# Another order around the biased score maps: scores earlier on PE, bias ahead of a division, even exponentials ahead of copies

## The reference, cut to what matters

```python
# a: 8 heads, plain softmax
sc = q @ k.T;  p = softmax(sc);  y = p @ v
# b: 8 heads, window of 128 keys to each side, bias by distance, and a sink
sc = where(valid, q @ k.T + bias, -1e30)
m  = max(max(sc, axis=-1), sink)
e  = exp(sc - m);  p = e / (sum(e) + exp(sink - m));  y = p @ v
# c: 4 heads with two maps each; the second is subtracted, scaled by lam
p = softmax(sc + bias);  y = (p[0] - lam * p[1]) @ v
...
gates  = sigmoid(h @ w_gates)            # 3 x 1024 columns
merged = sum over the three kinds of gates * (y @ w_branch)
```

## Time and profile before

| what | value |
|---|---|
| time, median of 3 executions | 2519.49 us (2513.41 to 2519.65) |
| the profiled execution: time / span | 2518.29 us / 2516.5 us |
| PE busy | 2479.6 us, 99% of the span |
| DVE, ACT, POOL busy | 1531.5, 1346.9, 255.5 us |
| DMA engines, share of the span on the main queue | 51.8% |
| chain that ended last, share by engine | PE 92%, DVE 4%, ACT 2%, issue 1% |

### The profile page before, as it was taken

One profiled execution on the slowest core, in us unless ns is written; L12 is line 12 of the kernel. 1 busy time (PEld: TensorE's weight loads), 2 busy tenths in 40 slices (PEclk: granted clock), 3 DMA queues, 4 the chain that ended last, 5 costly groups with the idle time before them and its releaser, 6 DMA issues.

```text
span 2516.5 us, 47973 instructions
## 1 busy us (share of the span) xinstructions
PE 2479.6 (99%) x19246; PEld 2312.7 (92%) x19246; DVE 1531.5 (61%) x2036; ACT 1346.9 (54%) x2077; POOL 255.5 (10%) x164
## 2 busy tenths in 40 slices
PE   9999999999999999999999999999999999999998
PEld 8989998999999999899989989799989988888997
DVE  5658756565565774656656556566555655567654
ACT  5447555544544664655555445665445445565543
POOL 0200220000000002100100001460000000354000
PEclk9999999999999999999999999999999999999999
DMA  6655414465655552348656555345555655434654
GB/s 235 207 186 172 136 67 160 143 197 195 198 198 193 168 166 70 126 142 228 205 178 202 194 177 161 110 145 187 188 189 186 195 193 168 135 111 167 201 188 139
DMA packets 118382, 428.10 MB, mean 170 GB/s; under 512 B 13164, under 2 KB 14956, under 8 KB 117804
## 3 DMA queue, kind: packets, MB, share of 16 engines
q1 hardware_dynamic: 117696, 424.82, 51.8%
q10 hardware_dynamic: 492, 0.46, 0.1%
HBM read 423.79 MB, written 1.44 MB: 169 GB/s over the span
## 4 chain that ended last, share of the span: by engine, by line
PE 92%; DVE 4%; ACT 2%; issue 1%; DMA 0%; ACTq 0%; SPq 0%; DVEq 0%; POOLq 0%
PE bank L483 41%; PE bank L694 39%; PE bank L503 2%; PE bank L1004 2%; PE bank L1708 1%; PE bank L1104 1%; DVE lo_slots L471 1%; PE bank L633 1%; PE bank L1725 1%; PE bank L1751 1%; PE bank L1895 1%; PE bank L1871 1%; DVE rope_mem L2108 1%; ACT hi_slots L457 0%; ACT probs L1790 0%
## 5 line engine op out<-in xcount | busy, mean ns | idle before, releaser
L471 DVE TENSOR_TENSOR lo_slots<-raw,hi_slots 128x1024 fp32r<-128x1024 f32 x732 | 901.1, 1237 | 696.3 <-ACT hi_slots L457 695.9
L457 ACT ACTIVATE hi_slots<-raw 128x1024 fp32r<-128x1024 f32 x788 | 830.7, 1058 | 737.2 <-PE bank L694 453.0
L694 PE MATMUL bank<-x_hi_room,hi_slots 128*128 128x256 f32 x2816 | 786.0, 279 | 1.7 <-DVE x_lo_room L663 1.2
L694 PE MATMUL bank<-x_lo_room,hi_slots 128*128 128x256 f32 x2816 | 784.1, 278 | 0.0
L694 PE MATMUL bank<-x_hi_room,lo_slots 128*128 128x256 f32 x2816 | 784.0, 278 | 0.0
L694 PEld LDWEIGHTS bank<-x_lo_room,hi_slots 128*128 128x128 f32 x2816 | 534.4, 190 | 0.1
L694 PEld LDWEIGHTS bank<-x_hi_room,hi_slots 128*128 128x128 f32 x2816 | 529.7, 188 | 3.9 <-issue 3.6
L694 PEld LDWEIGHTS bank<-x_hi_room,lo_slots 128*128 128x128 f32 x2816 | 530.0, 188 | 0.0
L483 PE MATMUL bank<-x_hi_room,hi_slots 128*128 128x256 f32 x1152 | 327.7, 285 | 1.9 <-DVE x_lo_room L663 1.4
L483 PE MATMUL bank<-x_lo_room,hi_slots 128*128 128x256 f32 x1152 | 319.7, 278 | 0.0
L483 PE MATMUL bank<-x_hi_room,lo_slots 128*128 128x256 f32 x1152 | 319.6, 277 | 0.0
(11 more groups left out here) (336 smaller groups left out, 3125.0 us busy)
## 6 DMA issues: line engine op xcount, KB each, us to landing
raw<-w_full SPq DMA_DIRECT2D x792, 512.0 KB, 4.1
bias_mem<-bias_rows SPq DMA_DIRECT2D x8, 288.0 KB, 6.4
mem<-mem_t SPq DMA_DIRECT2D x2, 1024.0 KB, 8.4
const<-consts SPq DMA_DIRECT2D x1, 1664.0 KB, 8.8
h<-x_t SPq DMA_DIRECT2D x2, 512.0 KB, 7.8
final<-finals SPq DMA_DIRECT2D x2, 512.0 KB, 6.4
out_t<-h SPq DMA_DIRECT2D x4, 256.0 KB, 2.7
bias_rows<-junk ACTq DMA_DIRECT2D x1, 384.0 KB
```

The source lines that it names most:

```text
L457: nc.scalar.activation(w_hi[s], raw[s][:, :], ACT.Copy).then_inc(hi_ready[s], 1)
L471: nc.vector.tensor_tensor(w_lo[s], raw[s][:, :], w_hi[s].bitcast(F32), ALU.subtract).then_inc(lo_ready[s], 1)
L694: mm = nc.tensor.matmul(out, lhsT=w[:, part], rhs=x[:, k, :], start=k == 0 and b % 2 == 0 and n == 0, stop=k == KT - 1 and b % 2 == 1 and ...
```

## The change

Three orders change; no instruction is added or taken away.

- PE: the scores of maps 10 and 11, 12 and 13, 14 and 15 (the pairs of b maps that follow a pair of b maps) are issued a step earlier, behind the values and ahead of that step's gate product.
- DVE: for the even maps 10, 12 and 14, the bias is added ahead of the division of the map before.
- ACT: at every even step, for all three kinds, the exponentials of map i come ahead of the copy of the transposed map and of the copy of the values.

```diff
         def pe_attention(E, maps):
             for i in range(len(maps) + 2):
-                if i < len(maps) and i % 2 == 0:
...
+                if i < len(maps) and i % 2 == 0 and not scores_early(maps, i):
+                    pe_scores(E, maps, i)
...
+                if scores_early(maps, i + 1):
+                    pe_scores(E, maps, i + 1)
                 for g in gates_at(E, i):
                     pe_gate(E, g)
...
+        def scores_early(maps, i):
+            return 2 <= i < len(maps) and i % 2 == 0 and maps[i - 1]["kind"] == maps[i]["kind"] == "b"
...
         def act_attention(E, maps):
+            for i in range(len(maps) + 3):
+                first = i % 2 == 0
+                if first:
+                    exponential(i)
+                turned(i)
+                values(i)
+                if not first:
+                    exponential(i)
                 for g in gates_at(E, i - 1):
                     act_gate(E, g)
...
         def dve_attention(E, maps):
             for i in range(len(maps) + 4):
+                if scores_early(maps, i):
+                    add_bias(i)
                 if 1 <= i <= len(maps):
...
...
-                    dve.wait_ge(sems["s_ps"], E.after("s_ps", i + 1))
-                    if m["kind"] in "bc":
...
+                    if m["kind"] == "a":
+                        dve.wait_ge(sems["s_ps"], E.after("s_ps", i + 1))
+                    else:
+                        if not scores_early(maps, i):
+                            add_bias(i)
```

More of the change, by code:

```diff
@@ L1692, in act_gate, with pe_scores @@
             split_hi(E, u)
+        def scores_early(maps, i):
+            return 2 <= i < len(maps) and i % 2 == 0 and maps[i - 1]["kind"] == maps[i]["kind"] == "b"
+        def pe_scores(E, maps, i):
+            two = maps[i:i + 2]
+            for n in range(i - 2 if i else 0, i):
+                if maps[n]["kind"] in "bc":
+                    pe.wait_ge(sems["s_bias"], E.after("s_bias", 2 * maps[n]["biased"] + 2))
+                else:
+                    pe.wait_ge(sems["s_exp"], E.after("s_exp", 2 * (n + 1)))
+            if i == 0:
+                pe.wait_ge(sems["pads"], E.after("pads", 1))
+            for t in range(TT):
+                for r, m in enumerate(two):
+                    mm = nc.tensor.matmul(bank[4 + r][:, tile_cut(t)], lhsT=m["q"][:, t * P:(t + 1) * P], rhs=m["k"],
+                                          start=True, stop=True)
+                    if t == TT - 1:
+                        mm.then_inc(sems["s_ps"], 1)
         def pe_attention(E, maps):
@@ L1762, in act_attention, with turned @@
             probs, probs_t, stat = attention_tiles(E)
-            for i in range(len(maps) + 3):
+            def turned(i):
                 if 1 <= i <= len(maps) and maps[i - 1]["use"] is not None:
@@ L1769, in act_attention, with values @@
                     nc.scalar.activation(probs_t[:, u % 2, :], bank[6 + u % 2][:, :], ACT.Copy).then_inc(sems["pt_sb"], 1)
+            def values(i):
                 if i >= 3 and maps[i - 3]["use"] is not None:
@@ L1780, in act_attention, with exponential @@
                                              ACT.Copy).then_inc(sems["y_hi"], 1)
+            def exponential(i):
                 if i < len(maps):
@@ L1805, in dve_attention, with add_bias @@
             probs, probs_t, stat = attention_tiles(E)
+            def add_bias(i):
+                m = maps[i]
+                dve.wait_ge(sems["s_ps"], E.after("s_ps", i + 1))
+                if i >= 3 and maps[i - 3]["use"] is not None:
+                    dve.wait_ge(sems["pt_ps"], E.after("pt_ps", maps[i - 3]["use"] + 1))
+                elif i >= 3:
+                    dve.wait_ge(sems["s_diff"], E.after("s_diff", maps[i - 3]["head"] - HEADS + 1))
+                for t in range(TT):
+                    at = (1 - t) * P
+                    nc.vector.tensor_tensor(probs[:, i % 3, tile_cut(t)], bias[:, m["head"], at:at + TOK],
+                                            bank[4 + i % 2][:, tile_cut(t)], ALU.add).then_inc(sems["s_bias"], 1)
             for i in range(len(maps) + 4):
+                if scores_early(maps, i):
+                    add_bias(i)
                 if 1 <= i <= len(maps):
```

## The result

Median of eight runs 2538.11 us (2529.61 to 2540.59), beside 2516.18 for eight runs of the kernel before (2510.16 to 2520.39). The ratio is 1.008, 95% interval 1.0062 to 1.0099: slower by 21.9 us. The profiled execution took 2540.00 with a span of 2538.1, 21.6 more than the span before.

The account below looks back on a forecast made before the run. It took TensorE to bound the kernel, the b stage being paced by VectorE's negated maximum held behind GpSimd's weight splits. 2.25 + 8.55 = 10.8 us a layer, 21.6 for two, on 2518.29 gave 2539.9, median 2540; range 2523 to 2545.

Parts of the forecast that it names:

- Early scores, nothing: Maps 10 to 15: earlier scores gain nothing, as GpSimd's split holds the even map's negated maximum; 6.1 us if nothing held.
- Bias ahead of the division, nothing: VectorE, even b maps: bias addition before the previous map's division costs nothing; PE regets some 0.3 at the next transpose.
- the upper end: 2544: delayed splits take 2.64, not 2.40 (1.9 us in all), and odd b transposes start 0.3 late (1.8 in all).
- b stage, 2.25 a layer: Maps 8 to 15: later splits hold the odd negated maximum, a pair takes 10.77 for 10.02; three pairs, +2.25 a layer.
- c stage, 8.55 a layer: Maps 16 to 23: splits hold division and then subtraction; 1.81 + 4.32 + 2.42 = 8.55 us a layer.
- its unknown: c stage: the order in which a waiting split and a waiting VectorE operation get their turn; full hold taken.
- a stage, nothing: Maps 0 to 7: the later split ends before the odd map's division and PE is not idle; no change.
- The waits of PE for the subtraction: c stage, sign to look for: PE waits about 2 us at maps 17, 19, 21 and 23.
- only the b stage loses: Rival: no split comes between the c stage's division and subtraction; 5.2 us slower in all, 2524; chance 0.11.
- Idle time gone: Rival: the change does what its order says and PE's idle time in b goes; 6.1 us faster, 2512; chance 0.07.

Follow-up runs that it names:

- E1: Changed kernel with ScalarE's order put back, leaving only early scores and early bias addition; ratio to the kernel before 1.0002, -3.2 us timed.
- E2: Changed kernel with scores and bias addition as before, leaving only even exponentials first at all maps; ratio to the kernel before 1.0095, +22.4 us.
- E4: Changed kernel with even exponentials first only in the c stage (maps 16, 18, 20, 22); ratio to the kernel before 1.0086, +19.5 us.
- E5: Changed kernel without the b stage's negated maximum, the sink left out of the maximum; one run, 2528.34 us.
- E3: Changed kernel with even exponentials first only in the b stage (maps 8, 10, 12, 14); ratio to the kernel before 1.0039, +9.1 us.
- E8: Changed kernel with tanh and weight split ahead of ScalarE's copies in the b stage, old order elsewhere; ratio to the kernel before 0.9991, -1.4 us.
- E6: E3 without the b stage's negated maximum, the sink left out of the maximum; ratio to the kernel before 0.9962, -9.8 us.
- E12: The same kernel as E8, run once more on another chip; ratio to the kernel before 0.9969, -6.0 us.

## Why the prediction was right

It said 2540, from 2518.29 for the profiled execution and 21.6 on top (on the median shown, 2519.49, the sum would have been 2541.1). Measured: 2538.11, and 2540.00 for the profiled execution, +21.6 in the span. The mechanism was right, the splits that end later and what they hold; that the last digit fits is luck, as the sum below shows. By its steps:

1. *Early scores, nothing*: E1, 39.8 in b as before. The reason holds as well: the negated maximum of the even map is held in its place. That an instruction that comes 0.5 us behind the start of a split waits for all of it decides this step.
2. *Bias ahead of the division, nothing*: E1 again, though PE's ten waits there are 9.0 in place of 8.5. The 1.8 us of the upper end did not come: E1's maps took 0.3 less than before.
3. *b stage, 2.25 a layer*: measured 2.16 and 2.26 (exponential 8 to 16); scores 16 came 42.26 behind scores 8, for 40.10. Exponentials 5.74 and 5.03 apart for 5.76 and 5.01.
4. *c stage, 8.55 a layer*: measured 8.28 and 8.18 (5.84 + 2.44 in layer 0, 5.83 + 2.35 in layer 1). Exponential 18 came 10.14 behind 16 for 10.23; transpose 17 came 8.78 behind exponential 16 for 8.85; transpose 23 8.50 behind exponential 22 for 8.58. The step called the order in which a waiting split and a waiting operation of VectorE get their turn its unknown. That was hardly put to the test: the second split was released at 1647.70, started 5.75 behind the exponential as forecast, and so was there 0.33 before the subtraction; what was decided is that the running second half of the division did not keep it out until then. All eight subtractions were held (2.64 to 2.75). The splits took 2.40 and 2.42 and not 2.64, so the 1.9 us of the upper end did not come.
5. *a stage, nothing*: it was 0.65 shorter in layer 0 and 0.39 in layer 1 (exponential 0 to 8), a small gain not forecast. With the negated maximum in place, the kernels with the old order in this stage took 35.4 to 35.7 and E2, with the new one, 35.0 (without it, 35.2 to 35.3 against 34.8), so the order gives 0.4 or so a layer and the rest of the 0.65 is spread. Why it gives that was not looked into.

The sum by stages is +19.8 and not 21.6: 1.0 less in the a stages, 0.6 less in the c stages and 0.1 less in b. What fills it up was not in the sum: 1.3 us between the layers' maps, 0.4 ahead of the first and 0.1 behind the last. That these cancel is luck, all the more as other executions differ by up to 12.5 us ahead of the first map and by some 4 between the layers. The 1.3 has a cause, and it is the clock.

The waits of PE for the subtraction were forecast as about 2.0 at each odd map: 1.74, 1.99, 0.47 and 2.78 in the rows above. The third is short because PE was late itself. Windows of one microsecond of the changed kernel, about transposes 19 and 23:

```profile
1661.00:1662.00 1.00, 1.00 (x5) 1.00 (x6) 0.96 (x3) 0.00 (x0) 0.00 (x0) 0.50 0.49 135
1662.00:1663.00 1.00, 1.00 (x7) 1.00 (x6) 0.26 (x1) 0.70 (x3) 0.00 (x0) 0.50 0.89 344
...
1682.00:1683.00 1.00, 1.00 (x7) 1.00 (x7) 0.00 (x0) 1.00 (x3) 0.00 (x0) 0.50 0.95 356
...
1685.00:1686.00 1.00, 1.00 (x10) 0.97 (x9) 0.00 (x0) 0.02 (x1) 1.00 (x1) 1.00 0.08 16
```

The granted clock is 0.50, the 1.2 GHz level, behind the waits of 1.99 and 2.78 us. Behind the first, the next wait swallows it. Behind the last there is none, and the branch product of 24 matmuls takes 4.26 in layer 0, where the clock fell, and 2.74 in layer 1, where it did not after a wait of the same length. The chain of the changed kernel, start and length:

```profile
1681.68 4.26 PE bank L483 x24
...
2294.90 2.74 PE bank L483 x24
```

So 1.5 us are lost there, once. In E2, E4 and E5 the same fell in layer 1, and the stretch behind the maps took 244.2 to 244.5 us in place of 243.1.

The rivals: *only the b stage loses* is what E3 does when the c order is kept, and not what the change does. *Idle time gone* is E5's b stage, without the instruction that is held. By the Trainium skill ("SBUF — State Buffer", "Who interferes with whom"), the one that issues first has the shared pair for its whole instruction, and a reduction never contends. The traces agree: 1.96 (E1) against 0.23 (E8) for the 128x2 instruction, and 0.69 for E6's reduction inside a split as outside of one.

## What to carry to other kernels

Where GpSimd works in the background, look for the short VectorE instructions on the path whose durations differ from call to call: the negated maximum took 1.15 and 0.32 us in the earlier trace rows and up to 1.97 in the changed kernel, and whoever moves work ahead of the instruction that releases GpSimd delays the end of GpSimd's work, and with it whatever that holds. An edit that brings an input earlier gains nothing while such an instruction ends at GpSimd's end; take it away first (E6), or trigger GpSimd earlier (E8, E12), and then the same edits pay. Judge a change of some microseconds by its stages in the trace; two sets of timed runs of one kernel, on two chips, had medians 4.6 us apart here.

## What the runs showed of the hardware that was not expected

- TensorE's granted clock fell to 0.50 inside a stretch where PE was busy 36 of 43 us, behind waits of 1.99 and 2.78 us, and not behind every such wait (2.78 in layer 1 of the changed kernel: none). It cost 1.5 us for 24 matmuls when nothing covered it.
- A GpSimd instruction that is released while a VectorE instruction runs gets in ahead of the next, dependent one: the split started 0.08 us behind its release and 0.33 before the subtraction, so that a chain of division and subtraction was held twice, 0.67 (1.29 less 0.62) and 1.90 us (2.65 less 0.75).
- A fill by GpSimd, which reads nothing, also held the 128x2 instruction, to 0.02 us of its end.
